# Eight transfer buffers and an unrolled sum, or four buffers and loops: the modulation prologue of a two-layer transformer kernel

## The reference

```
mod = silu(c) @ w_ada + b_ada                 # w_ada: 2048 x 6144
shift, scale, gate = split(mod, 3)
h = rms_norm(x, g_norm) * (1 + scale) + shift
proj = h @ w_in                               # first large matrix product
... attention of two kinds, gating, w_out, a second mixer layer, an FFN of 5632 x 2 ...
```

## Time and profile before

| what | us |
|---|---|
| median of three executions (2107.04 to 2111.60) | 2108.87 |
| the profiled execution, device time | 2107.04 |
| its span, from the first to the last instruction | 2105.2 |
| PE busy in it | 1991.2 (95%) |
| DVE busy in it | 1281.6 (61%) |

### The profile page before, as it was taken

One profiled execution on the slowest core, in us unless ns is written; L12 is line 12 of the kernel. 1 busy time (PEld: TensorE's weight loads), 2 busy tenths in 40 slices (PEclk: granted clock), 3 DMA queues, 4 the chain that ended last, 5 costly groups with the idle time before them and its releaser, 6 DMA issues.

```text
span 2105.2 us, 38795 instructions
## 1 busy us (share of the span) xinstructions
PE 1991.2 (95%) x15084; PEld 1889.0 (90%) x15084; DVE 1281.6 (61%) x1565; ACT 989.8 (47%) x1429; POOL 144.6 (7%) x151
## 2 busy tenths in 40 slices
PE   4289999999999999999999998999999999999997
PEld 2189999999998999988989998899999999988885
DVE  7886886675666544444457654655665665654544
ACT  3055555555644544444445454644444444444443
POOL 0000000000002000000004221000000000000000
PEclk8599999999999999999999999999999999999998
DMA  9966665575555566545444555366566656655553
GB/s 376 349 210 235 245 200 159 168 273 157 158 183 154 174 177 178 162 140 146 143 139 153 191 186 170 92 184 183 171 185 185 180 176 185 205 188 185 186 189 120
DMA packets 179903, 391.62 MB, mean 186 GB/s; under 512 B 11955, under 2 KB 17632, under 8 KB 177376
## 3 DMA queue, kind: packets, MB, share of 16 engines
q1 hardware_dynamic: 178800, 388.03, 58.0%
q10 hardware_dynamic: 1024, 2.51, 0.3%
HBM read 388.39 MB, written 2.10 MB: 185 GB/s over the span
## 4 chain that ended last, share of the span: by engine, by line
PE 90%; DVE 6%; ACT 2%; issue 1%; DMA 1%; SPq 0%; DVEq 0%; POOLq 0%; POOL 0%; ACTq 0%
PE acc L761 20%; PE acc L762 20%; PE acc L763 20%; PE psum_y L762 2%; PE psum_x L761 2%; PE psum_x L763 2%; PE psum_y L763 2%; PE psum_y L761 2%; PE psum_x L762 2%; DVE ada_acc L1665 2%; PE acc L1131 2%; PE acc L1130 2%; PE acc L1129 2%; DMA ada_w<-in_w_ada 1%; DVE ada_first L1665 1%
## 5 line engine op out<-in xcount | busy, mean ns | idle before, releaser
L1671 DVE TENSOR_TENSOR w_lo<-raw,w_hi 128x1024 fp32r<-128x1024 f32 (+1 forms) x644 | 813.5, 1271 | 712.6 <-ACT w_hi L1178 709.0
L1178 ACT ACTIVATE w_hi<-raw 128x1024 fp32r<-128x1024 f32 (+1 forms) x644 | 675.2, 1050 | 899.0 <-PE acc L763 580.5
L761 PE MATMUL acc<-act_hi,w_lo 128*128 128x258 f32 (+2 forms) x3424 | 978.5, 286 | 17.2 <-issue 9.3
L762 PE MATMUL acc<-act_lo,w_hi 128*128 128x258 f32 (+2 forms) x3424 | 968.3, 283 | 0.0
L763 PE MATMUL acc<-act_hi,w_hi 128*128 128x258 f32 (+2 forms) x3424 | 968.0, 283 | 0.0
L761 PEld LDWEIGHTS acc<-act_hi,w_lo 128*128 128x128 f32 x3424 | 651.8, 190 | 28.1 <-issue 26.6
L762 PEld LDWEIGHTS acc<-act_lo,w_hi 128*128 128x128 f32 x3424 | 651.1, 190 | 0.7 <-issue 0.5
L763 PEld LDWEIGHTS acc<-act_hi,w_hi 128*128 128x128 f32 x3424 | 650.6, 190 | 0.0
L762 PE MATMUL psum_y<-act_lo,w_hi 128*128 128x258 f32 x352 | 100.7, 286 | 0.0
L761 PE MATMUL psum_x<-act_hi,w_lo 128*128 128x258 f32 x352 | 100.4, 285 | 0.0
L763 PE MATMUL psum_x<-act_hi,w_hi 128*128 128x258 f32 x352 | 100.3, 285 | 0.0
(11 more groups left out here) (293 smaller groups left out, 2186.1 us busy)
## 6 DMA issues: line engine op xcount, KB each, us to landing
raw<-in_w_in SPq DMA_DIRECT2D x272, 512.0 KB, 3.7
raw<-in_w_ffn_up SPq DMA_DIRECT2D x176, 512.0 KB, 3.8
raw<-in_w_ffn_down SPq DMA_DIRECT2D x88, 512.0 KB, 3.6
raw<-in_w_out SPq DMA_DIRECT2D x64, 512.0 KB, 4.2
raw<-in_w_ada SPq DMA_DIRECT2D x32, 512.0 KB, 8.4
ada_w<-in_w_ada SPq DMA_DIRECT2D x32, 512.0 KB, 8.3
ada_x<-in_w_ada SPq DMA_DIRECT2D x16, 1024.0 KB, 6.4
raw<-in_w_attn_o SPq DMA_DIRECT2D x16, 512.0 KB, 3.6
```

What stands on the lines that cost most here:

```text
L761: pe.matmul(out, w_lo, a_hi, start=c == 0, stop=False)
L762: pe.matmul(out, w_hi, a_lo, start=False, stop=False)
L1178: act.activation(M.hi[s][:, 0:job.width], M.raw[s][:, 0:job.width], ACT.Copy).then_inc(M.hi_ready[s], 1)
L1671: dve.tensor_tensor(M.lo[s][:, 0:job.width], M.raw[s][:, 0:job.width], M.hi[s][:, 0:job.width].bitcast(FP32), ALU.subtract).then_inc(M.lo_ ...
```

## The change

The sum uses the four `raw` buffers alone, with the semaphores that the weight stream uses anyway (`raw_in`, `lo_ready`), and both sides are rolled: per group one round of four pieces is written out, and three more rounds are a loop with the piece number in a register. The count of landings in the later panels starts at 16 per buffer, the first projection piece in buffer s waits for the last prologue piece in the same buffer, and SP's wait for 60 pieces is gone. All other code is the same.

```
-    counts = {"raw": 0, "hi": 0, "used": [0] * 4, "ready": [0] * 4, "free": [0] * 4}
+    counts = {"raw": 16, "hi": 0, "used": [0] * 4, "ready": [0] * 4, "free": [0] * 4}
...
-    for n in range(4 * DC):
-        g, k = n // DC, n % DC
-        at_least(sp, M.adaw_used, n - 7)
-        sp.dma_start(M.ada_w[n % 8][:, :], w_ada[k, g // 2, g % 2]).then_inc(M.adaw_in[n % 8], 16)
+    for g in range(4):
+        def ada_rows(i, uses):
+            for s in range(SLOTS):
+                at_least(sp, M.lo_ready[s], uses)
+                sp.dma_start(M.raw[s][:, :], w_ada[ds(4 * i + s, 1), g // 2, g % 2]
+                             .rearrange("k p c -> p (k c)")).then_inc(M.raw_in[s], 16)
+
+        ada_rows(0, 4 * g)
+        with sp.Fori(0, DC // 4 - 1) as i:
+            ada_rows(i + 1, i + 1 + 4 * g)
...
-    sp.wait_ge(M.adaw_used, 4 * DC - 4)
...
-        pe.wait_ge(M.adaw_used, DC * (g + 1))
+        pe.wait_ge(M.lo_ready[3], 4 * (g + 1))
...
-        for k in range(DC):
-            n = DC * g + k
-            dve.wait_ge(M.adaw_in[n % 8], 16 * (n // 8 + 1))
-            if k > 0:
-                dve.wait_ge(M.adaw_used, n)
-            stt(part, M.ada_w[n % 8][:, :], M.silu_c[:, k:k + 1], part, ALU.mult, ALU.add
-                ).then_inc(M.adaw_used, 1)
+        def rows_summed(i):
+            for s in range(SLOTS):
+                dve.wait_ge(M.raw_in[s], 16 * (i + 4 * g + 1))
+                if s > 0:
+                    dve.wait_ge(M.lo_ready[s - 1], i + 4 * g + 1)
+                else:
+                    at_least(dve, M.lo_ready[3], i + 4 * g)
+                stt(part, M.raw[s][:, :], M.silu_c[:, ds(4 * i + s, 1)], part, ALU.mult, ALU.add
+                    ).then_inc(M.lo_ready[s], 1)
+
+        rows_summed(0)
+        with dve.Fori(0, DC // 4 - 1) as i:
+            rows_summed(i + 1)
```

More of the change, by code:

```diff
@@ L182, in memory @@
     M.lo = [put(f"w_lo{s}", [P, PIECE], F32R) for s in range(SLOTS)]
-    M.ada_w = [*M.raw, *(put(f"ada_w{s}", [P, PIECE], offset=base + (8 + s) * PIECE * 4) for s in range(SLOTS))]
     M.rT = put("rT", [P, DC * ROWS])
@@ L403, in memory @@
     M.val_free = [sem(f"val_free{s}") for s in range(4)]
-    M.adaw_in = [sem(f"adaw_in{n}") for n in range(8)]
-    M.adaw_used = sem("adaw_used")
     M.ada_in = [sem(f"ada_in{n}") for n in range(2)]
```

## The result

| kernel | median us | lowest to highest | runs |
|---|---|---|---|
| before | 2110.21 | 2107.04 to 2111.60 | 4 |
| after | 2128.89 | 2125.35 to 2132.55 | 4 |

The ratio is 1.0093, with a 95% interval of 1.0078 to 1.0108: 18.7 us slower. The forecast was +4.5 us and 2113.4, and the range ended at 2119: the prediction was wrong, the loss is four times what it said. The later rounds with the experiments have more executions of both kernels: there the median of the kernel after is 2128.76 (21 executions in all), that of the kernel before 2110.95 to 2111.70, so the loss is rather 17 to 18 us than 19. The profiled execution of the kernel after took 2125.42 us against 2107.04, with a span of 2123.6 against 2105.2: +18.4.

The account below looks back on a forecast made before the run. DVE's sum, not transfers, was taken to set PE's start. Loops 3.6+0.5, piece 7 0.1, seams 0.6, hole -0.3 make +4.5 us; on the median 2108.87 that is 2113.4, range 2107.5 to 2119.

Parts of the forecast that it names:

- First the four buffers: In the sum's weight stream, a round of four takes 5.2 us against DVE's 5.9, so fewer buffers cost nothing.
- alone 3.6, in line 1.3: Price of one weight transfer: 3.6 us when it stands alone, 1.3 us when it stands in line.
- the value falls all the time, which a floor wouldn't: Argument that landings of 4.9 to 5.1 us at the stream's end were a remaining queue, against too few buffers.
- The first rival: In the sum's stream, four buffers are too few: 1.67 us a piece, +16 us, 2125; chance 0.17.
- Second, the loops: On DVE's looped sums, the separate wait and register step add 0.11 or 0.045 us a piece: 3.6 and 0.5 us.
- the register work is hidden: Rival on DVE's looped sums: spacing stays 1.39 us, +0.2 us in all, 2109.1; chance 0.14.
- Third and fourth, the seams and the hole at 52.1 us: On DVE, three groups' first pieces now wait, +0.6 us; a 0.42 us idle hole may go, taken -0.3.
- The start: First pieces of the sum: issue of pieces 0 to 3 unchanged, piece 4 issued at 10.76 us; no change.
- that rival: At the sum's start, pieces 1 to 7 come up to 3.1 us earlier, giving 2110.3 or 2106.0; chance 0.09.
- it comes in line as now: At the sum's start, piece 4 lands behind the pieces before it, which land by 15.4 us, without delay.
- Fifth, the end: After the sum, the first projection piece is issued 1.4 us later but covered by 3.6 us: costs nothing.
- Sixth, the first panel: Panel behind the sum: paced by DVE, it moves as a whole and gives none of the delay back.

Follow-up runs that it names:

- experiment 1: The kernel before with 4 instead of 8 pieces of the sum's weights outstanding, straight code, eight buffers kept: 2126.58 us, ratio 1.0065.
- experiment 3: The kernel before with 8, 1, 2 and 3 pieces outstanding in groups 0 to 3, straight code; not timed, spacings 5.09, 2.89 and 1.99 us in groups 1 to 3.
- experiment 12: The kernel before with 5 instead of 8 pieces outstanding, straight code: 2112.44 us, ratio 1.0005.
- experiment 4: The kernel before with 4, 5, 6 and 7 pieces outstanding in groups 0 to 3; not timed, spacings 1.785, 1.459, 1.389 and 1.389 us.
- experiment 6: The kernel before with two groups summed in turn, so a sum waits for the one before the last; eight buffers, straight code: 2105.36 us, ratio 0.9973.
- experiment 2: The kernel before with groups 1 to 3 as loops of eight pieces on SP and DVE, eight buffers kept: 2116.94 us, ratio 1.0023.
- experiment 9: The kernel after, its four buffers and loops kept, with each piece as two half transfers and two half sums on different columns: 2114.25 us, ratio 1.0012 to before.
- experiment 8: The kernel before cut to four raw buffers, straight code, each half piece transferred, waited for, summed and given back by itself: 2110.28 us, ratio 0.9998.
- experiment 5: The kernel before with 4 pieces outstanding, straight code, ACT issuing every second piece from number 17 on: 2128.51 us, ratio 1.0084.

## Why the prediction was wrong

**The failing step: "First the four buffers".** It put the round at 0.16+3.6+0.14+1.28 = 5.2 us and its cost at nothing. Three of the four numbers stand in the chain of the kernel after nearly as they were put: 0.16 on SP, 0.13 (53.14 to 53.27) before a looped sum behind its landing, 1.28 of work. The fourth, the landing, is 5.3 instead of 3.6, so the round is 0.16+5.3+0.14+1.28 = 6.9 us and a piece takes 1.72. Measured were 1.77, 1.72 and 1.71 in groups 1 to 3. With the loops' part in it, that is 82.55-66.68 = 15.9 us over these 48 pieces, and group 0 adds 3.0. The depth alone, put at nothing, costs 14.9 (experiment 1). The condition that the prediction gave, that the buffers decide if a landing takes over 4.3 us, was met.

Why 3.6 was the wrong price: the first transfer of the earlier trace rows and those of the earlier trace rows had little or nothing beside them (at 1300 to 1600 us the share is 0.55, the rate 163 GB/s), and the 5.7 that the earlier trace rows also show was left out. The straight kernels give the price at each load; the last column is the round worked out, (landing + 0.03 + 0.1 + 1.28) divided by the depth, with the 0.1 for the gap behind a landing:

| depth | DMA share | GB/s | landing us | spacing us | worked out |
|---|---|---|---|---|---|
| 1 | 0.36 | 109 | 3.8 | 5.09 | 5.21 |
| 2 | 0.64 | 200 | 4.3 | 2.89 | 2.86 |
| 3 | 0.83 | 281 | 4.6 | 1.99 | 2.00 |
| 4 | 0.92 | 315 | 5.0 to 5.5 | 1.65 to 1.75 | 1.60 to 1.73 |
| 5 | 0.98 | 367 | 5.5 | 1.42 to 1.44 | 1.38, DVE 1.39 |
| 6, 7 | 1.01, 1.02 | 402, 410 | 5.3 to 6.2 | 1.389 | up to 1.27, DVE 1.39 |

(Landings and spacings by group, of experiments 3, 1, 12 and 4.) One buffer of n is in DVE's hands most of the time, so at depth 4 about three transfers share the engines (5.3/1.72 = 3.1). The prediction took "alone 3.6, in line 1.3" as if nothing lay between: below a full queue a landing should have been 3.6. But company costs before there is a queue. Share divided by rate is the time that the engines are busy for a byte; for a piece (0.524 MB) it is 1.73 us at depth 1 (0.36/109), 1.68 at depth 2, 1.55 at 3, 1.53 at 4, 1.40 at 5, and with a full queue 1.32 (experiment 6, share 1.03 at 409 GB/s). In these runs the engines were at their best only where more was always waiting.

The argument "the value falls all the time, which a floor wouldn't" was the slip in reasoning. The falling part was a queue, as the prediction said, but it falls to a floor: in experiment 2 the landings are down to 5.5 at 57 us and are still 5.5 at 84 to 100 us. The 4.9 to 5.1 at the end of the old stream were already near it.

**The first rival was the true one.** "Four buffers are too few" said 1.67 a piece, +16, 2125; measured 1.71 to 1.77, +18.7, 2128.9. It had 0.17. The loops' part of about 2 us is inside the measured +18.7, so the rival's agreement in size is good to some us, not better. The Trainium skill (DMA: Bandwidth & Descriptors, Latency and other measured facts) puts the memory's latency at 0.2 us on average and 2 us at high load, and the estimate from it, 1.75 a piece and 2129, was the closest in the text. The runs agree with the size of the step, 1.5 to 1.7 us against 1.8 between the Trainium skill's two figures (3.8 us alone and 5.3 to 5.5 near the full load); that the memory is the place, no run here shows, so this closeness may be luck.

**The other steps.**
- Second, the loops: right. 0.21 in place of 0.105 between looped sums, 1.43 onto the first of a round, and +5.3 us for experiment 2, where the terms of the prediction come to 42 x 0.11 + 3 x 0.045 + 3 x (0.19+0.045) = 5.5 (48 looped pieces, of which six begin a round and three of these a group). In the trace of that kernel the 48 pieces take 4.7 us more than before, and the hole of 0.4 is gone. At depth 4 the loops don't add up in full: 82.55-80.35 = 2.2 us over the 48 pieces, 119.53-117.79 = 1.7 at the sum's end and 2128.76-2126.58 = 2.2 by the medians (18.7-14.9 = 3.8 compares two rounds in which the kernel before differed by 1.45), since a piece that waits for its landing hides the step. The rival "the register work is hidden" fell for a sum that waits for the one before it; experiment 9 shows that the work is hidden where none does.
- Third and fourth, the seams and the hole at 52.1 us: tenths, lost between landings in the kernel after, not tested alone. The hole is gone in experiment 2, where no gap in groups 1 to 3 is over 0.22, and is there in the straight code of experiment 12 (0.53).
- The start: right for piece 1, wrong behind it. Piece 1 starts at 12.64 (12.67 before) behind the same 1.93 us of idle time, so pieces 4 to 7 were not what it waited for, and that rival falls. But "it comes in line as now" was too kind: piece 7 starts at 22.33 instead of 21.71 and piece 8 at 24.19 instead of 23.10, 1.1 us late instead of 0.1 to 0.2. The cause is again the landing: the transfers issued one by one from 10.89 on take 4.5 us and more, not 3.6.
- Fifth, the end: right. ACT rounds the first projection piece at 120.01, done at 121.07, and DVE wants it at 123.77.
- Sixth, the first panel: right. +18.83 ahead of it is +18.82 at its start and +18.4 at the end.

**How it divides.** Depth 14.9 us (experiment 1, interval 10 to 18), loops on top of it about 2. With eight buffers the loops alone cost 5.3. The depth's part is not the price of less memory but of handling it 512 KB at a time: in halves, the same four buffers lose nothing (experiment 8).

**What stays open.** Why a transfer keeps the engines busier for its bytes when little else is queued; the trace gives the busy share, not what an engine waits for inside it. What pays in experiment 8, the earlier start of a sum or the earlier return of its buffer. The 2 us of experiment 9 behind its sum.

## What to carry to other kernels

Count the buffers that can be in transfer, which is one less than there are while the consumer holds one, and price a landing at the load that it will run at: landings taken from a stretch with little traffic are too short. If memory must shrink, try smaller pieces, each waited for and given back by itself, before fewer ones. A running sum that waits for itself pays a gap each time (0.105 us here), and a loop makes it twice as long; sums in turn, each waiting for the one before the last, paid neither here, whole pieces in straight code and halves in a loop.

## What the runs showed of the hardware

- The time from issue to landing of 512 KB grows well below a full queue: 3.8 us at a DMA share of 0.36, 4.3 at 0.64, 4.6 at 0.83 (experiment 3), 5.3 at 0.89 (the kernel after), 5.5 at 0.96 (experiment 2).
- A share near 1 is not full speed: 0.89 brought 304 GB/s, 0.98 brought 367, and 1.02 brought 410. Per unit of share the engines bring 109/0.36 = 303, 304/0.89 = 342 and 410/1.02 = 402 GB/s with pieces of 512 KB, and 386/1.05 = 368 with halves (experiment 8).
- Two issuing engines instead of one did not bring the spacing at depth 4 down to DVE's 1.39: 1.63 and 1.71 us in groups 2 and 3, against 1.68 and 1.75 (experiments 5 and 1).
- A looped sum that waits for the one before it starts 0.21 us after it, a straight one 0.105, and one that waits for the last but one follows without a gap (4 in 5.12 us), in straight code; half sums in a loop come at the spacing of straight ones (0.68 and 0.69).
